# In every weight step, the matmuls that read rounded weights run first, and the wait for the weights' remainder moves behind them

## The chip, the cores and the metric

One Trainium2 chip, of which the kernel uses one core. The metric is the device time of one execution in microseconds (us): the median of several runs, lower is better. The profile describes one further execution of the same program.

## The reference

One layer of a streaming encoder for 256 tokens of width 4096, in float32. The input is normalised and multiplied by one large matrix `w_in` (4096 x 21504) whose columns feed two branches: attention in a sliding window of chunks with 16 heads, and an HGRN2 gated recurrence with 16 heads. Each branch has a SiLU gate. Both are projected up to the model width, merged by sigmoid gates, projected once more, added to the input and normalised:

```python
h = rmsnorm(x, norm_gain[l])
proj = jnp.einsum('bsd,dn->bsn', h, w_in[l])
qa, ka, va, za, qb, fb, ib, zb, ga, gb = jnp.split(proj, SPLIT_POINTS, axis=-1)
a = window_sink_attention(qa, ka, va, attn_sinks[l]) * jax.nn.silu(za)
ob = hgrn2_chunkwise(qb, fb, ib, lower_bounds[l])
...
y = (jax.nn.sigmoid(ga) * jnp.einsum('bsc,cd->bsd', a, w_up_attn[l])
     + jax.nn.sigmoid(gb) * jnp.einsum('bsc,cd->bsd', b, w_up_hgrn[l]))
x = x + jnp.einsum('bsd,de->bse', y, w_out[l])
return rmsnorm(x, final_norm_gain)
```

Nearly all of the work is in these matrix products: some 0.5 GB of weights are read once.

## The kernel before, in words

**Weight steps.** All products with large matrices are cut into weight steps. A step takes one tile of weights, 128 rows of the contraction by 512 columns, and multiplies it with all 256 tokens. There are 1856 steps, numbered through the whole program. To keep the precision of float32 with the faster float32r matmul, both operands are split into a rounded part and a remainder, and a step makes three products: rounded by rounded, remainder of the activations by rounded weights, rounded activations by the weights' remainder. The tokens are two tiles of 128 (`TT` = 2, the stationary operand `l_hi` or `l_lo`), the weights are the moving operand (`w_hi`, `w_lo`, 512 columns). So a step is six matmuls (`step_r`, lines L399 to L401), each accumulating into one PSUM bank of 512 columns per token tile; 16 or 32 steps fill one output block of 512 columns.

**How a tile of weights gets there.** SyncE (SP) fetches two tiles with one DMA into the ring `raw` of four slots (`load_steps`, L316). ScalarE (ACT) copies a tile with rounding to `w_hi` (`round_step`, L596) and signals `hi_ready`; it waits for the DMA and for TensorE to have finished the step four places earlier (`pe_done`), since `w_hi` and `w_lo` are rings of four (`RING`). VectorE (DVE) waits for `hi_ready`, subtracts `w_hi` from `raw` and writes `w_lo` (`rest_step`, L856), and signals `lo_ready`. TensorE (PE) waits for `lo_ready` before the first matmul of the step. `lo_ready` also lets SP refill `raw`.

**What stands between the steps.** Every engine has one queue in order, and the program writes by hand at which step k of a block which side work goes. TensorE transposes finished rows (`turn`, L411), and makes the small matmuls of the heads. In an HGRN head (32 steps; `hgrn_side`), TensorE computes level scores behind k = 14 and k = 18 (L419, L421) and the head's output behind k = 22 (L441 to L443), for which it waits for `att_done`, among others. VectorE masks the scores at k = 16 and 20 (L927) and sums them in one long reduction `at_m` at k = 17 and 21 (L934), behind the `rest_step` of the same k. There are 16 such heads in four groups; their side work runs beside the steps numbered 128 to 639. After them come keys and values, the attention heads (16 steps each), the merge with its gates and up projections, and the output projection (`project`), which adds the residual. In its first block VectorE also makes `h_lo` of the merged rows (L1138).

**Signals of a step.** The last matmul of a step signals `pe_done`. In the last step of a block of the output projection, the third product of token tile 0 also signals `tile0_done`, so that VectorE can add the residual of that half (`residual`, L1122) while the second half is still being multiplied. In the blocks within the projection the residual stands behind `rest_step` of k = 3 of the next block; the last block's residual stands behind nothing but the wait. After it come squares (L831), the final norm and the stores.

**Loops.** The first HGRN group and some blocks between phases are written out; the rest runs in loops, 16 iterations in all. In a loop the value that a wait compares with depends on the iteration: `count` gives an expression of the loop's register, and the engine works it out with a register instruction.

**In the diff:** `step_t` is a second form of the step, called from nowhere. `step_r` is called by `hgrn_group`, the last HGRN block, `attn_blocks`, `merge` and `project`.

Of the kernel before, what the change touches and what calls it, by code (L numbers as in the profile page):

```python
# [30 lines left out]
P = 128  # L31
# [7 lines left out]
SEQ = 256  # L39
TT = SEQ // P  # L40
D = 4096
KT = D // P
HD = 128
HEADS = 16
KVH = 4
GH = 4
# [3 lines left out]
BLK = GH * HD  # L50
# [41 lines left out]
RING = 4  # L92
# [13 lines left out]
def count(base, per=0, it=0):  # L106

    def c(k=0, unit=1):
        if isinstance(it, int):
            return (base + per * it + k) // unit  # L110
        assert per % unit == 0
        return it * (per // unit) + (base + k) // unit
    return c


def build(nc, x, norm_gain, w_in, attn_sinks, lb_logits, hgrn_norm_gain, w_up_attn, w_up_hgrn,
          w_out, final_norm_gain, tables, out):
    ctx = ExitStack()
    with ctx:
        def sb(name, shape, dt=F32):  # L120
            return ctx.enter_context(nc.sbuf_tensor(name, shape, dt))

        def sem(name):
            return ctx.enter_context(nc.semaphore(name))
# [3 lines left out]
        w_hi = sb("w_hi", [P, RING, BLK], F32R)  # L128
        w_lo = sb("w_lo", [P, RING, BLK], F32R)
# [78 lines left out]
        acc = ctx.enter_context(nc.psum_tensor("acc", [P, 2, 2 * BLK], F32))  # L208
# [6 lines left out]
        hi_ready = sem("hi_ready")  # L215
        lo_ready = sem("lo_ready")
        pe_done = sem("pe_done")
# [154 lines left out]

        @block.tensor
        def _(pe):
            def step_t(n, k, par, r_hi, r_lo, kt, last, free):

                s = k % RING
                if kt == 0 and free is not None:
                    pe.wait_ge(*free)
                pe.wait_ge(lo_ready, n(k + 1))  # L380
                for c in range(GH):
                    o = acc[:, par, c * SEQ:(c + 1) * SEQ]
                    cols = slice(c * HD, (c + 1) * HD)
                    first = kt == 0 and c % 2 == 0
                    nc.tensor.matmul(o, w_hi[:, s, cols], r_hi[:, kt, :], start=first, stop=False)
                    nc.tensor.matmul(o, w_hi[:, s, cols], r_lo[:, kt, :], start=False, stop=False)
                    m = nc.tensor.matmul(o, w_lo[:, s, cols], r_hi[:, kt, :], start=False, stop=last and c % 2 == 1)
                m.then_inc(pe_done, 1)

            def step_r(n, k, par, l_hi, l_lo, kt, last, free, rows_done=None):  # L390

                s = k % RING
                if kt == 0 and free is not None:
                    pe.wait_ge(*free)
                pe.wait_ge(lo_ready, n(k + 1))
                for t in range(TT):
                    o = acc[:, par, t * BLK:(t + 1) * BLK]
                    tok = slice(t * P, (t + 1) * P)
                    nc.tensor.matmul(o, l_hi[:, kt, tok], w_hi[:, s, :], start=kt == 0, stop=False)  # L399
                    nc.tensor.matmul(o, l_lo[:, kt, tok], w_hi[:, s, :], start=False, stop=False)  # L400
                    m = nc.tensor.matmul(o, l_hi[:, kt, tok], w_lo[:, s, :], start=False, stop=last)  # L401
                    if last and t == 0 and rows_done is not None:
                        m.then_inc(rows_done, 1)
                m.then_inc(pe_done, 1)
# [82 lines left out]
            def hgrn_group(n, g, hd, nt, side):  # L487


                before = [(i_copied, g), (silu_done, g * 2), (sig_f_done, g + 1), (silu_done, g * 2 + 1)]  # L490
                for b in range(4):
                    free = before[b] if side or b >= 2 else None
                    for k in range(KT):
                        kk = b * KT + k
                        if not side and b == 0 and k % 2 == 0:
                            pe.wait_ge(h_lo_done, k // 2 + 1)
                        step_r(n, kk, b % 2, h_hi, h_lo, k, k == KT - 1, free)
                        if k == 16 and (side or b) and b < 3:

                            turn((b - 1) % 2, turn_h, nt(b))  # L500
                        if side:
                            hgrn_side(k, lambda i, b=b: hd(b + i))
                        elif b == 0 and k % 2 == 0 and k // 2 + 3 < KT // 2:
                            input_pair(k // 2 + 3)
# [10 lines left out]
            n = count(N_HG)  # L515
            before = [(i_copied, GROUPS), (silu_done, 2 * GROUPS), (kv_copied, 1), (kv_copied, 2)]
            for b in range(4):
                for k in range(KT):
                    kk = b * KT + k
                    free = before[b]  # L520
                    step_r(n, kk, b % 2, h_hi, h_lo, k, k == KT - 1, free)
                    if k == 16 and b != 2:
                        turn((b - 1) % 2, turn_h, 3 * GROUPS + {0: 0, 1: 1, 3: 2}[b])
                    hgrn_side(k, lambda i, b=b: (GROUPS - 1) * GH + b + i)


            def attn_blocks(n, hd, g, nt):
                before = [(qa_copied, g + 1), (silu_done, g + (2 * GROUPS + 1))]
                for b in range(2):
                    for k in range(KT):  # L530
                        kk = b * KT + k
                        step_r(n, kk, b % 2, h_hi, h_lo, k, k == KT - 1, before[b])
                        if k == 7:

                            turn((b - 1) % 2, turn_a, nt(b + 1))
                        attn_side(k % 16, lambda i, u=kk // 16: hd(u + i), g)
# [681 lines left out]
```

## Time and profile before

| | us |
|---|---|
| median of 3 runs | 2707.37 |
| lowest and highest | 2707.24, 2707.83 |
| the profiled execution, its own time | 2707.25 |
| its span, first to last instruction | 2704.7 |
| TensorE busy in matmuls (PE) | 2672.3 |
| weight loads (PEld, beside PE) | 2219.0 |
| VectorE busy (DVE) | 1609.3 |
| ScalarE busy (ACT) | 1452.1 |

Times on the timeline count from the span's start. A timeline row gives start, duration, engine, line and operation, and in brackets how long the engine was idle before and what released it; "x3" is several like instructions in a row. PE are the matmuls, PEld the loads of the stationary operand, which run beside the matmul before. The end of a matmul is modelled and matmuls are pipelined, so their rows overlap: each lasts 0.39 us although the next starts 0.23 us after it. What a standstill costs is therefore read from the starts. "issue" is time in which an engine waited for nothing that the profile shows.

### The profile page before, as it was taken

How to read it: one execution, taken by the hardware profiler on the slowest of the kernel's cores; microseconds unless marked ns; L12 is line 12 of the kernel's file. 1: busy time of each engine (PE TensorE's matmuls, PEld its weight loads, DVE VectorE, ACT ScalarE, POOL GpSimd, SP SyncE). 2: the span in 40 equal slices, each digit the busy share in tenths (PEclk: the TensorE clock that was granted, in tenths of full speed). 3: DMA queues.
4: the chain of work that ended last, by engine and by line, in shares of the span. 5: the costliest groups of instructions: out<-in, count | busy, mean ns of one | idle time of the engine just before them, and what ended most of it. 6: DMA issues, size and time to landing. Idle time of an engine off the chain costs nothing.

```text
span 2704.7 us, 39969 instructions
## 1 busy us (share of the span) xinstructions
PE 2672.3 (99%) x12249; PEld 2219.0 (82%) x12249; DVE 1609.3 (59%) x3037; ACT 1452.1 (54%) x2418; POOL 0.2 (0%) x4
## 2 busy tenths in 40 slices
PE   8999999999999999999999999999999999999997
PEld 7888888888888888888888888888888888888886
DVE  6457777777777765555555555555555555655554
ACT  6556565565565555555654444444444444554444
POOL 0000000000000000000000000000000000000000
PEclk9999999999999999999999999999999999999999
DMA  7665555565555556656666666666666666666665
GB/s 238 193 187 171 162 175 168 163 179 163 164 178 157 175 168 178 178 171 180 177 189 192 194 188 192 193 190 191 193 192 189 194 188 194 203 215 204 215 213 182
DMA packets 258914, 503.06 MB, mean 186 GB/s; under 512 B 15552, under 2 KB 15760, under 8 KB 258832
## 3 DMA queue, kind: packets, MB, share of 16 engines
q1 hardware_dynamic: 258608, 502.02, 61.6%
q8 instruction: 41, 0.67, 0.1%
q14 instruction: 41, 0.34, 0.0%
q10 hardware_dynamic: 224, 0.03, 0.0%
HBM read 497.80 MB, written 4.19 MB: 186 GB/s over the span
## 4 chain that ended last, share of the span: by engine, by line
PE 95%; DVE 2%; issue 1%; DMA 0%; ACT 0%; SPq 0%; DVEq 0%; ACTq 0%
PE acc L399 30%; PE acc L401 30%; PE acc L400 30%; PE lev L419 1%; DVE lev_m L927 1%; DVE w_lo L856 1%; PE acc L411 1%; DVE at_m L934 1%; PE lev L421 0%; DMA x_in<-in_x_dram 0%; PE lev L547 0%; PE mis L447 0%; PE mis L432 0%; PE lev L456 0%; PE mis L461 0%
## 5 line engine op out<-in xcount | busy, mean ns | idle before, releaser
L856 DVE TENSOR_TENSOR w_lo<-raw,w_hi 128x512 fp32r<-128x512 f32 x1856 | 1260.7, 689 | 918.7 <-ACT w_hi L596 918.3
L596 ACT ACTIVATE w_hi<-raw 128x512 fp32r<-128x512 f32 x1856 | 1146.9, 630 | 1027.6 <-PE acc L401 1012.3
L399 PE MATMUL acc<-w_hi,h_hi 128*128 128x512 f32 x3200 | 1267.3, 396 | 7.2 <-DVE w_lo L856 6.4
L401 PE MATMUL acc<-w_lo,h_hi 128*128 128x512 f32 x3200 | 1247.9, 390 | 0.0
L400 PE MATMUL acc<-w_hi,h_lo 128*128 128x512 f32 x3200 | 1246.4, 390 | 0.0
L399 PEld LDWEIGHTS acc<-w_hi,h_hi 128*128 128x128 f32 x3200 | 601.4, 188 | 136.2 <-DVE w_lo L856 14.9
L401 PEld LDWEIGHTS acc<-w_lo,h_hi 128*128 128x128 f32 x3200 | 600.9, 188 | 127.8
L400 PEld LDWEIGHTS acc<-w_hi,h_lo 128*128 128x128 f32 x3200 | 601.5, 188 | 120.3
L399 PE MATMUL acc<-w_hi,a_hi 128*128 128x512 f32 x256 | 99.6, 389 | 0.0
L400 PE MATMUL acc<-w_hi,a_lo 128*128 128x512 f32 x256 | 99.6, 389 | 0.0
L401 PE MATMUL acc<-w_lo,a_hi 128*128 128x512 f32 x256 | 99.6, 389 | 0.0
L399 PE MATMUL acc<-w_hi,b_hi 128*128 128x512 f32 x256 | 99.6, 389 | 0.0
L400 PE MATMUL acc<-w_hi,b_lo 128*128 128x512 f32 x256 | 99.6, 389 | 0.0
L401 PE MATMUL acc<-w_lo,b_hi 128*128 128x512 f32 x256 | 99.6, 389 | 0.0
L934 DVE TENSOR_REDUCE at_m<-lev_m 128x128 f32<-128x1024 f32 x32 | 63.8, 1993 | 0.0
L927 DVE TENSOR_TENSOR lev_m<-mis,tab 128x64 f32<-128x64 f32 x32 | 7.2, 225 | 89.1 <-PE lev L421 89.1
L399 PEld LDWEIGHTS acc<-w_hi,b_hi 128*128 128x128 f32 x256 | 48.1, 188 | 10.0
L399 PEld LDWEIGHTS acc<-w_hi,a_hi 128*128 128x128 f32 x256 | 48.1, 188 | 10.0
L400 PEld LDWEIGHTS acc<-w_hi,a_lo 128*128 128x128 f32 x256 | 48.1, 188 | 10.0
L400 PEld LDWEIGHTS acc<-w_hi,b_lo 128*128 128x128 f32 x256 | 48.1, 188 | 10.0
L401 PEld LDWEIGHTS acc<-w_lo,a_hi 128*128 128x128 f32 x256 | 48.1, 188 | 9.9
L401 PEld LDWEIGHTS acc<-w_lo,b_hi 128*128 128x128 f32 x256 | 48.1, 188 | 9.9
(156 smaller groups left out, 1067.8 us busy)
## 6 DMA issues: line engine op xcount, KB each, us to landing
raw<-in_w_in_dram SPq DMA_DIRECT2D x672, 512.0 KB, 3.7
raw<-in_w_out_dram SPq DMA_DIRECT2D x128, 512.0 KB, 3.9
raw<-in_w_up_attn_dram SPq DMA_DIRECT2D x64, 512.0 KB, 3.6
raw<-in_w_up_hgrn_dram SPq DMA_DIRECT2D x64, 512.0 KB, 3.6
xr<-in_x_dram SPq DMA_DIRECT2D x8, 512.0 KB, 4.6
out_dram<-xr SPq DMA_DIRECT2D x6, 512.0 KB, 4.8
x_in<-in_x_dram SPq DMA_DIRECT2D x2, 1024.0 KB, 10.7
fgain<-in_final_norm_gain_dram SPq DMA_DIRECT2D x8, 256.0 KB, 5.9
```

What stands on the lines that cost most here:

```text
L399: nc.tensor.matmul(o, l_hi[:, kt, tok], w_hi[:, s, :], start=kt == 0, stop=False)
L400: nc.tensor.matmul(o, l_lo[:, kt, tok], w_hi[:, s, :], start=False, stop=False)
L401: m = nc.tensor.matmul(o, l_hi[:, kt, tok], w_lo[:, s, :], start=False, stop=last)
L411: m = nc.tensor.transpose(acc[:, par, c * SEQ + t * P:c * SEQ + (t + 1) * P], rows_sb[:, t, c * P:(c + 1) * P], ident)
L419: nc.tensor.matmul(level_scores(t, i), decay[:, i - 1, tok], late_half(decay[:, i - 1, tok], i), start=True, stop=True)
L596: nc.scalar.activation(w_hi[:, k % RING, :], raw[:, (k // 2) % RING, k % 2, :], ACT.Copy).then_inc(hi_ready, 1)
L856: nc.vector.tensor_tensor(w_lo[:, k % RING, :], raw[:, (k // 2) % RING, k % 2, :], w_hi[:, k % RING, :].bitcast(F32), ALU.subtract).then_i ...
L927: nc.vector.tensor_tensor(late_half(lev_m[:, i, :], i), level_scores(t, i), own, ALU.mult)
L934: nc.vector.tensor_reduce(at_m[:, t, :], lev_m[:, :, :].rearrange("p l t -> p t l"), AX_X, ALU.add).then_inc(att_done, 1)
```

## The change

The unused `step_t` goes. In `step_r` the wait for `lo_ready` ahead of the six matmuls becomes a wait for `hi_ready`. The order of the matmuls changes: first, for token tile 0 and then for tile 1, the two that read `w_hi`; then the wait for `lo_ready`; then the two that read `w_lo`, tile 0 and tile 1. `tile0_done` stays on the `w_lo` matmul of tile 0, which is now the fifth and not the third, `pe_done` on the last. Nothing changes on the other engines.

```diff
         def _(pe):
-            def step_t(n, k, par, r_hi, r_lo, kt, last, free):
+            def step_r(n, k, par, l_hi, l_lo, kt, last, free, rows_done=None):
 
                 s = k % RING
                 if kt == 0 and free is not None:
                     pe.wait_ge(*free)
-                pe.wait_ge(lo_ready, n(k + 1))
-                for c in range(GH):
...
-                m.then_inc(pe_done, 1)
-
-            def step_r(n, k, par, l_hi, l_lo, kt, last, free, rows_done=None):
-
-                s = k % RING
-                if kt == 0 and free is not None:
-                    pe.wait_ge(*free)
-                pe.wait_ge(lo_ready, n(k + 1))
-                for t in range(TT):
-                    o = acc[:, par, t * BLK:(t + 1) * BLK]
-                    tok = slice(t * P, (t + 1) * P)
+                outs = [(acc[:, par, t * BLK:(t + 1) * BLK], slice(t * P, (t + 1) * P)) for t in range(TT)]
+                pe.wait_ge(hi_ready, n(k + 1))
+                for o, tok in outs:
                     nc.tensor.matmul(o, l_hi[:, kt, tok], w_hi[:, s, :], start=kt == 0, stop=False)
                     nc.tensor.matmul(o, l_lo[:, kt, tok], w_hi[:, s, :], start=False, stop=False)
+                pe.wait_ge(lo_ready, n(k + 1))
+                for t, (o, tok) in enumerate(outs):
                     m = nc.tensor.matmul(o, l_hi[:, kt, tok], w_lo[:, s, :], start=False, stop=last)
                     if last and t == 0 and rows_done is not None:
                         m.then_inc(rows_done, 1)
```

## Rows read from the trace of the kernel before

**Rows 1.** The page: busy time by engine, and the granted clock in 40 slices

```profile
PE 2672.3 (99%) x12249; PEld 2219.0 (82%) x12249; DVE 1609.3 (59%) x3037; ACT 1452.1 (54%) x2418; POOL 0.2 (0%) x4
...
PEclk9999999999999999999999999999999999999999
```

**Rows 2.** The page: the chain that ended last; a costly group of instructions

```profile
PE 95%; DVE 2%; issue 1%; DMA 0%; ACT 0%; SPq 0%; DVEq 0%; ACTq 0%
PE acc L399 30%; PE acc L401 30%; PE acc L400 30%; PE lev L419 1%; DVE lev_m L927 1%; DVE w_lo L856 1%; PE acc L411 1%; DVE at_m L934 1%; PE lev L421 0%; DMA x_in<-in_x_dram 0%; PE lev L547 0%; PE mis L447 0%; PE mis L432 0%; PE lev L456 0%; PE mis L461 0%
...
L856 DVE TENSOR_TENSOR w_lo<-raw,w_hi 128x512 fp32r<-128x512 f32 x1856 | 1260.7, 689 | 918.7 <-ACT w_hi L596 918.3
```

**Rows 3.** Timeline of TensorE's matmuls: start us, us, engine, line, operation; two stretches

```profile
120.21 0.39 PE L399 MATMUL acc<-w_hi,h_hi 128*128 128x512 f32 x1
...
121.57 0.39 PE L399 MATMUL acc<-w_hi,h_hi 128*128 128x512 f32 x1
...
1499.97 0.39 PE L399 MATMUL acc<-w_hi,h_hi 128*128 128x512 f32 x1
...
1501.33 0.39 PE L399 MATMUL acc<-w_hi,h_hi 128*128 128x512 f32 x1
```

**Rows 4.** List of waits: engine, line <- releaser: us in total, times, longest us

```profile
PEld acc L399 <- DVE w_lo L856: 14.9, 21, 0.7
...
PE acc L399 <- DVE w_lo L856: 6.4, 21, 0.3
...
PEld lev L483 <- DMA x_in<-in_x_dram: 4.2, 1, 4.2
...
PEld acc L399 <- issue: 1.8, 2, 1.2
```

**Rows 5.** Waits of the weight loads, from 200 to 400 us

```profile
PEld acc L399 <- DVE w_lo L856: 3.6, 5, 0.7
```

**Rows 6.** Instructions of line L934: count, ns min/median/max, first and last start

```profile
L934 DVE TENSOR_REDUCE at_m<-lev_m x32: 1976/2000/2004, 221.1 to 976.6; 128x128 f32<-128x1024 f32 x32
```

**Rows 7.** Timeline of step k = 22 of one head, all engines

```profile
228.88 2.00 DVE L934 TENSOR_REDUCE at_m<-lev_m 128x128 f32<-128x1024 f32 x1
...
230.80 1.88 DVE L856 TENSOR_TENSOR w_lo<-raw,w_hi 128x512 fp32r<-128x512 f32 x3
230.83 0.39 PE L401 MATMUL acc<-w_lo,h_hi 128*128 128x512 f32 x1
231.53 0.19 PEld L399 LDWEIGHTS acc<-w_hi,h_hi 128*128 128x128 f32 x1 [0.74 <-DVE w_lo L856]
231.53 0.50 PE L399 MATMUL acc<-w_hi,h_hi 128*128 128x512 f32 x1 [0.31 <-DVE w_lo L856]
...
231.87 0.40 PE L400 MATMUL acc<-w_hi,h_lo 128*128 128x512 f32 x1
```

**Rows 8.** Timeline of step k = 18 of the last head of a group

```profile
373.28 0.50 PE L399 MATMUL acc<-w_hi,h_hi 128*128 128x512 f32 x1 [0.29 <-DVE w_lo L856]
```

**Rows 9.** Timeline of two places in the output projection

```profile
2344.94 0.47 PE L399 MATMUL acc<-w_hi,h_hi 128*128 128x512 f32 x1 [0.23 <-DVE w_lo L856]
...
2345.25 0.39 PE L400 MATMUL acc<-w_hi,h_lo 128*128 128x512 f32 x1
...
2424.64 0.39 PE L401 MATMUL acc<-w_lo,h_hi 128*128 128x512 f32 x1
...
2424.90 0.50 PE L399 MATMUL acc<-w_hi,h_hi 128*128 128x512 f32 x1
```

**Rows 10.** Timeline of VectorE behind the last weight step

```profile
2688.46 1.29 DVE L1122 TENSOR_TENSOR xr<-xr,acc 128x512 f32<-128x512 f32 x2 [3.47 <-PE acc L401]
```

**Rows 11.** Timeline: weight loads of eight transposes; the next weight load starts at 1006.44

```profile
1005.44 1.03 PEld L411 LDWEIGHTS acc<-tab,turn_a 128*128 128x128 f32 x8
```

**Rows 12.** Timeline of the first weight step of the kernel

```profile
13.27 0.63 PE L400 MATMUL acc<-w_hi,h_lo 128*128 128x512 f32 x1
13.70 0.63 PE L401 MATMUL acc<-w_lo,h_hi 128*128 128x512 f32 x1
```

More of the change, by code:

```diff
@@ L374, in _ @@
         def _(pe):
-            def step_t(n, k, par, r_hi, r_lo, kt, last, free):
-                s = k % RING
-                if kt == 0 and free is not None:
-                    pe.wait_ge(*free)
-                pe.wait_ge(lo_ready, n(k + 1))
-                for c in range(GH):
[L382 to L387, printed above, removed]
-                m.then_inc(pe_done, 1)
             def step_r(n, k, par, l_hi, l_lo, kt, last, free, rows_done=None):
```

## The prediction

> **What bounds the kernel now.** I read the page's busy table and its 40 slices first: TensorE is busy for 99% of the span, at a granted clock of nine tenths or more in every slice, while VectorE has 59% and ScalarE 54% [rows 1]. The chain that ended last says the same of the order: 95% of the span lies on TensorE, 90% on the three matmul lines of the weight step [rows 2]. So only two things can move the time: how fast matmuls follow each other, and the moments at which TensorE stands still. A matmul's row lasts 0.39 us, but its end is modelled and the rows overlap, so the pace is in start times. In the timeline a matmul of 512 columns starts 0.23 us after the one before it; six of them, one weight step, take 1.36 us (120.21 to 121.57) [rows 3]. 1856 steps of 1.36 us are 2524 us of the 2704.7 us span.
>
> The standstills are in the list of waits. For the weights' remainder TensorE waited 21 times: 14.9 us by its weight loads, 6.4 us by its matmuls, at most 0.7 us at once [rows 4]. The longest single one of all is 4.2 us, for the input at the very start [rows 4]. Neither total is the cost: the weight load normally starts a matmul early, so its wait counts that lead too, and the matmul's begins only at a modelled end of 0.39 us. The cost is again in start times, below.
>
> **What the change removes.** A step now waits for w_lo before its first matmul, though only the third and sixth read it. After the change the first four wait for w_hi alone, and the wait for w_lo stands 4 x 0.23 = 0.91 us later. Where w_lo is late by less, nothing waits.
>
> Between 200 and 400 us there are five [rows 5], and the three stretches of 200 us up to 1000 us have five each too: twenty in all, where the HGRN heads run. Each head has two VectorE reductions at_m of 2.0 us (32 for 16 heads [rows 6]), and VectorE's queue is in order, so the next w_lo stands behind them. In one head the second reduction runs from 228.88 to 230.88; the w_lo behind it starts by about 230.8 and takes 1.88/3 = 0.63 us or a little more; TensorE, whose last matmul started at 230.83, starts the next at 231.53 [rows 7]. That is 0.70 us where 0.23 is usual, so 0.47 lost. The next start comes at 231.87, 0.34 us later: the weight load for it could not be brought forward either, another 0.11. After that the spacing is 0.23 again. One such wait costs **0.58 us**. Each of the 16 heads has one like it, at its step k = 22. Four more, one per group of heads, stand behind the first reduction (k = 18): there the matmul stood idle for 0.29 us behind the modelled end of the one before it [rows 8], where it is 0.31 in [rows 7], so I take 0.02 less, 0.56 us. Sum: 16 x 0.58 + 4 x 0.56 = **11.5 us**.
>
> Two stand in the output projection [rows 9]. The matmul at 2344.94 was idle for 0.23 us behind a modelled 0.39, 0.62 from start to start, and the next starts at 2345.25, 0.31 later: (0.62 - 0.23) + (0.31 - 0.23) = 0.47 us. From 2424.64 to 2424.90 it is 0.26, which with the 0.11 behind it is 0.14 us. Together **0.6 us**; 12.1 us in all.
>
> Does the later wait really pass? Without the stall the step of [rows 7] would start at 231.06, its fifth matmul at 231.97, and that matmul's weight load one matmul earlier, at 231.74. TensorE saw w_lo by 231.53. So 0.2 us is left over even for the weight load, and for k = 18 slightly more. The w_hi that now stands first is there: a w_lo is the difference of raw and w_hi, and the three w_lo from 230.80 follow each other without a pause (1.88 us for three [rows 7]), so their w_hi had been waiting. The next thing to be late is att_done, which the small matmuls behind that step need: the reduction ends at 230.88 and they would start at 232.4, so 1.5 us are left. The w_lo of the following step comes 0.6 us after the late one and is needed at least 1.36 us later. VectorE, with 59% busy, catches up from there as it does now.
>
> **What it moves.** In the last step of an output block the third matmul of token tile 0 signals tile0_done. It goes from third to fifth place: 2 x 0.227 = 0.45 us later. Within the projection the residual that waits for it stands behind a w_lo that needs the whole block finished, so nothing changes there. At the very end nothing covers it: VectorE, idle for 3.47 us before, begins the residual at 2688.46 when TensorE's line L401 lets it, and runs its two instructions in 1.29 us [rows 10]; squares, norm and stores follow one after the other. With the signal 0.45 us later, all of that moves by **+0.45 us**. pe_done keeps its place at the sixth matmul, so rounding, the refill of the weight ring and the DMA queue of SP see no change but the earlier pace; the order of accumulation alternates between the two PSUM halves more often (four changes of half per step and not two), and the existing changes are free: the start after one half's last matmul comes 0.23 us later like all others [rows 3].
>
> **What it adds.** 1856 waits for hi_ready, and in the loops a register instruction for each that works out the value. No view counts these as busy. From below: nothing, since the wait that is there costs nothing: a step in the written-out first group (120.21 to 121.57) and one in a loop, where the value is computed (1499.97 to 1501.33), both take 1.36 us [rows 3]. A gain from an added instruction is excluded. From above: TensorE's queue gets through eight weight loads and eight transposes from 1005.44 to 1006.44 [rows 11], 1.00/16 = 0.06 us an instruction. If two more per step were fully exposed, they would cost 1856 x 0.12 = some 220 us. I take nothing, by the nearest row: at 0.06 us each, the 12 instructions of a step and its wait with the register operation need 0.9 us of 1.36, and two more fit in what is left.
>
> **The sum.** -11.5 - 0.6 + 0.45 = -11.7 us. The profiled execution took 2707.25 us (span 2704.7), so 2695.6 us; the median of the runs, 2707.37, stands 0.1 us above it, which gives **2695.6** to 2695.7. About 0.2% (5.4 us, that is a bound of 2702.0) is what a measurement of this kernel tells from no change.
>
> The Trainium skill (TensorE: Matmul & The Clock Gate, section "Architectural detail: the array is 16× 32×32, not 1× 128×128") says that TensorE may pull weight loads ahead of running matmuls. If that reached past a semaphore wait, the load in [rows 7] would not have waited with its matmul and the 0.11 would not be part of the stall; it starts at the same 231.53 as the matmul, so here it does not, and the sum by the rule (some 2.3 us less gain, 2698) is not the one I take.
>
> **The rivals.**
> *A part of the stall stays* (chance 0.09): w_lo is in time for the matmul but the wait in the middle of a step has a restart of its own. If it cost the 0.11 of [rows 7] in the 20 heads' waits the time is 2698; if the load had to be released a further 0.3 us earlier, some 6 us of the gain would go, 2702. For it: only 0.2 us are left. Against it: the wait at a step's start shows no cost when it is met in time.
> *No change* (0.07): what is gained in a head is lost again, because VectorE is still behind and the next wait takes over, or the instruction stream pauses as it does once near 795 us, in a standstill of 1.2 us that the list calls "issue" [rows 4]. Time 2703 to 2708. Against it: 918.3 us of VectorE's idle time is spent waiting for w_hi [rows 2], so it has time to catch up between reductions.
> *Slower* (0.04): the added wait and its register instruction are not hidden in every step. It decides from 11.7/1856 = 0.006 us a step on; at one exposed instruction of 0.06 us per step it is +111 - 12, 2806 us. Against it: [rows 3], where the wait that exists adds nothing in either kind of step.
> *The clock* (0.01): TensorE's pace falls to its lower level of 1.2 GHz. The first matmuls after the idle start are 0.43 us apart and not 0.23 [rows 12]. Sixty matmuls at 0.43 would eat the gain, and all 11136 of them would give some 4900 us. The standstills of today leave every slice at nine tenths or more [rows 1], the mark of the upper level of 2.4 GHz, and the change has fewer of them. The Trainium skill (TensorE: Matmul & The Clock Gate, section "A second HAM failure mode: psum-queue depth-cycling") tells of a kernel whose cycling through PSUM banks idled TensorE briefly and let the clock swing; the changed order does cycle more, but no gap shows at a change of bank here.
>
> **How the numbers follow.** Forecast 0.79 at 2695.6. The range reaches from 2694.0 (the same sum with 1.6 us more, a few ordinary gaps or the pause near 795 us gone) to 2700.5, which takes in the nearer half of the first rival. Faster by over 0.2%: 0.79 and nearly all of 0.09, 0.88. Within: 0.07. Slower: 0.05, the last two rivals.
>
> **What would show it.** Right: the wait of line acc's weight load for w_lo gone from the list between 200 and 1000 us; TensorE's span from first to last matmul some 12 us shorter; steps still 1.36 us; the final residual starting after the fifth matmul of the last step and ScalarE's squares 0.45 us later behind it. Wrong: new waits of the third line for w_lo with a length of tenths, steps of more than 1.36 us in the loops, or standstills at the small matmuls behind k = 22 that are not there now.

## The result, and the profile after the change

| | before, us | after, us |
|---|---|---|
| median | 2707.30 (6 runs, 2706.85 to 2707.83) | 2694.57 (6 runs, 2693.36 to 2697.06) |
| the profiled execution, its own time | 2707.25 | 2693.91 |
| its span | 2704.7 | 2692.1 |

The ratio of the medians is 0.9953, with a 95% interval of 0.9942 to 0.9964: 12.7 us less, where 11.7 were forecast (2695.6).

The page of the changed kernel, with the lines that answer to [rows 1] and [rows 2]. The `w_hi` matmuls are now L383 and L384, the `w_lo` matmul L387; ScalarE's `w_hi` is L582 and VectorE's `w_lo` L842.

```profile
span 2692.1 us, 39969 instructions
...
PE 2665.9 (99%) x12249; PEld 2220.7 (82%) x12249; DVE 1608.6 (60%) x3037; ACT 1452.1 (54%) x2418; POOL 0.2 (0%) x4
...
PEclk9999999999999999999999999999999999999998
...
PE 99%; DMA 0%; ACT 0%; DVE 0%; SPq 0%; issue 0%; ACTq 0%; DVEq 0%
PE acc L383 31%; PE acc L384 31%; PE acc L387 31%; PE lev L405 1%; PE acc L397 1%; PE lev L407 0%; DMA x_in<-in_x_dram 0%; PE lev L533 0%; PE mis L433 0%; PE mis L418 0%; PE lev L442 0%; PE mis L447 0%; PE outp L428 0%; PE outp L452 0%; PE outp L453 0%; PE outp L429 0%
...
L842 DVE TENSOR_TENSOR w_lo<-raw,w_hi 128x512 fp32r<-128x512 f32 x1856 | 1259.9, 688 | 909.6 <-ACT w_hi L582 909.1
```

VectorE and ScalarE do the same work; the granted clock stays at nine tenths or more but for the last slice (an 8, of which the last 16 us lie behind the last matmul). Two things are to be seen here. TensorE's modelled busy time is only 6 us less, though the span is 12.6 us shorter: busy time does not show where the gain is, since it had been a matter of standstills. And the chain that ended last, which before had 2% on VectorE and 1% without a releaser, is 99% TensorE. VectorE's share there is now rounded to 0%.

The list of waits of the weight loads answers to [rows 4]. The wait for `w_lo`, 14.9 us in 21 times, is not in it at all:

```profile
PEld outp L458 <- DMA vrow<-in_hgrn_norm_gain_dram: 3.5, 1, 3.5
PEld lev L469 <- DMA x_in<-in_x_dram: 3.5, 1, 3.5
PEld mis L469 <- DMA x_in<-in_x_dram: 2.9, 1, 2.9
PEld acc L384 <- issue: 1.1, 1, 1.1
```

What is left is the input at the start and one pause of 1.1 us for which the profile names no cause; before, there was a like one of 1.2 us.

The timeline of the same head as in [rows 7]; the start times are this execution's own:

```profile
228.61 2.00 DVE L920 TENSOR_REDUCE at_m<-lev_m 128x128 f32<-128x1024 f32 x1
...
230.54 1.88 DVE L842 TENSOR_TENSOR w_lo<-raw,w_hi 128x512 fp32r<-128x512 f32 x3
...
230.79 0.39 PE L383 MATMUL acc<-w_hi,h_hi 128*128 128x512 f32 x1
...
231.47 0.39 PE L384 MATMUL acc<-w_hi,h_lo 128*128 128x512 f32 x1
231.48 0.41 PEld L387 LDWEIGHTS acc<-w_lo,h_hi 128*128 128x128 f32 x2
231.70 0.62 PE L387 MATMUL acc<-w_lo,h_hi 128*128 128x512 f32 x2
```

The reduction of 2.0 us is there as before, and the late `w_lo` behind it again starts before the reduction's end is over (the first of the three from 230.54). But the step starts at 230.79, with `w_hi`, and its load of the fifth matmul starts at 231.48, on the heels of the fourth matmul at 231.47: it has not waited. The `w_lo` matmuls follow at 231.70, 0.23 us later. The wait for `w_hi`, which now comes first, is met long before: ScalarE has ended this step's `w_hi` 4.6 us before the step's first matmul. The smallest such lead of all steps is 0.84 us (step 1662, in the output projection), the next 1.07 (step 6, at the start).

The end of the kernel, where [rows 10] had VectorE start 0.18 us ahead of the last matmul (2688.46 against 2688.64):

```profile
2675.36 0.61 PE L387 MATMUL acc<-w_lo,h_hi 128*128 128x512 f32 x2
2675.86 1.28 DVE L1108 TENSOR_TENSOR xr<-xr,acc 128x512 f32<-128x512 f32 x2 [3.92 <-PE acc L387]
2676.58 0.63 ACT L817 ACTIVATE sq_o<-xr 128x512 f32<-128x512 f32 x1 [3.86 <-DVE xr L1108]
```

The two `w_lo` matmuls start at 2675.36 and, 0.23 us later, at 2675.59; VectorE starts at 2675.86, now 0.27 us behind the last.

**Where the 12.6 us went**, from start times in both traces, cut at the same matmuls (counted from the kernel's first; the pieces are stretches of the same instructions):

| stretch | before, us | after, us | difference |
|---|---|---|---|
| span's start to matmul 49 (input, first steps) | 21.52 | 21.26 | -0.26 |
| matmul 49 to 4001 (to about 863 us) | 841.80 | 832.07 | -9.73 |
| 4001 to 8001 | 866.27 | 863.88 | -2.39 |
| 8001 to 10601 (all in the merge) | 585.72 | 585.72 | 0.00 |
| 10601 to the last (end of the merge, output projection) | 373.33 | 372.66 | -0.67 |
| last matmul to the span's end | 16.08 | 16.53 | +0.45 |

The four stretches between the start and the tail carry -12.8 us. The second profiled execution of the changed kernel has the same (832.03, 863.88, 585.72, 372.66 and 16.54 us). One thing in the stretch up to matmul 4001 is not the change's: every profiled execution has a pause there, ahead of the fourth matmul of step 512, the first step behind the loop over the head groups. The list puts it down to "issue". Before:

```profile
794.41 0.39 PE L401 MATMUL acc<-w_lo,h_hi 128*128 128x512 f32 x1
795.59 0.50 PE L399 MATMUL acc<-w_hi,h_hi 128*128 128x512 f32 x1 [0.78 <-issue]
```

From start to start it is 1.17 us before and 1.09 after, and between 0.76 and 1.88 us in the ten profiled executions of this study. Where stretches of different kernels are compared below, its difference is taken out first; here it leaves 9.65 of the 9.73 us to the change. In the merge, where no `w_lo` was late, nothing changed to a hundredth of a microsecond, although each of its steps has one wait more and four changes of PSUM half, not two.

### The profile page after: what moved, and what is told of

Same layout as the page of the kernel before. It is cut to its first block, busy times and chain, and to the rows that moved or that the text cites. A ratio compares the mean times of both kernels' runs of the same rounds, so it can differ in the third digit from the quotient of the medians.

```text
span 2692.1 us, 39969 instructions
## 1 busy us (share of the span) xinstructions
PE 2665.9 (99%) x12249; PEld 2220.7 (82%) x12249; DVE 1608.6 (60%) x3037; ACT 1452.1 (54%) x2418; POOL 0.2 (0%) x4
## 4 chain that ended last, share of the span: by engine, by line
PE 99%; DMA 0%; ACT 0%; DVE 0%; SPq 0%; issue 0%; ACTq 0%; DVEq 0%
PE acc L383 31%; PE acc L384 31%; PE acc L387 31%; PE lev L405 1%; PE acc L397 1%; PE lev L407 0%; DMA x_in<-in_x_dram 0%; PE lev L533 0%; PE mis L433 0%; PE mis L418 0%; PE lev L442 0%; PE mis L447 0%; PE outp L428 0%; PE outp L452 0%; PE outp L453 0%; PE outp L429 0%
## 5 line engine op out<-in xcount | busy, mean ns | idle before, releaser
L842 DVE TENSOR_TENSOR w_lo<-raw,w_hi 128x512 fp32r<-128x512 f32 x1856 | 1259.9, 688 | 909.6 <-ACT w_hi L582 909.1
L582 ACT ACTIVATE w_hi<-raw 128x512 fp32r<-128x512 f32 x1856 | 1147.1, 630 | 1024.3 <-PE acc L387 1008.2
L383 PE MATMUL acc<-w_hi,h_hi 128*128 128x512 f32 x3200 | 1265.4, 395 | 0.0
L384 PE MATMUL acc<-w_hi,h_lo 128*128 128x512 f32 x3200 | 1247.2, 390 | 0.7 <-issue 0.7
L387 PE MATMUL acc<-w_lo,h_hi 128*128 128x512 f32 x3200 | 986.9, 390 | 0.0
L387 PEld LDWEIGHTS acc<-w_lo,h_hi 128*128 128x128 f32 x3200 | 601.0, 188 | 127.2
L384 PEld LDWEIGHTS acc<-w_hi,h_lo 128*128 128x128 f32 x3200 | 601.5, 188 | 122.1 <-issue 1.1
L383 PEld LDWEIGHTS acc<-w_hi,h_hi 128*128 128x128 f32 x3200 | 601.4, 188 | 120.6
L383 PE MATMUL acc<-w_hi,a_hi 128*128 128x512 f32 x256 | 99.6, 389 | 0.0
L383 PE MATMUL acc<-w_hi,b_hi 128*128 128x512 f32 x256 | 99.6, 389 | 0.0
L384 PE MATMUL acc<-w_hi,a_lo 128*128 128x512 f32 x256 | 99.6, 389 | 0.0
L384 PE MATMUL acc<-w_hi,b_lo 128*128 128x512 f32 x256 | 99.6, 389 | 0.0
L387 PE MATMUL acc<-w_lo,a_hi 128*128 128x512 f32 x256 | 78.8, 389 | 0.0
L387 PE MATMUL acc<-w_lo,b_hi 128*128 128x512 f32 x256 | 78.8, 389 | 0.0
L383 PEld LDWEIGHTS acc<-w_hi,b_hi 128*128 128x128 f32 x256 | 48.1, 188 | 10.0
L383 PEld LDWEIGHTS acc<-w_hi,a_hi 128*128 128x128 f32 x256 | 48.1, 188 | 10.0
L384 PEld LDWEIGHTS acc<-w_hi,a_lo 128*128 128x128 f32 x256 | 48.1, 188 | 10.0
L384 PEld LDWEIGHTS acc<-w_hi,b_lo 128*128 128x128 f32 x256 | 48.1, 188 | 10.0
L387 PEld LDWEIGHTS acc<-w_lo,a_hi 128*128 128x128 f32 x256 | 48.1, 188 | 9.9
L387 PEld LDWEIGHTS acc<-w_lo,b_hi 128*128 128x128 f32 x256 | 48.1, 188 | 9.9
```

The source lines that it names most:

```text
L582: nc.scalar.activation(w_hi[:, k % RING, :], raw[:, (k // 2) % RING, k % 2, :], ACT.Copy).then_inc(hi_ready, 1)
L842: nc.vector.tensor_tensor(w_lo[:, k % RING, :], raw[:, (k // 2) % RING, k % 2, :], w_hi[:, k % RING, :].bitcast(F32), ALU.subtract).then_i ...
```

## The experiments

In the runs below the kernel before had medians of 2707.52 and 2707.62 us (15 runs in each of the two sets, 2705.6 to 2710.3), and the times are to be seen beside these.

### The changed kernel again

> The changed kernel again, beside the others on the same chip. Theory: 12.7 us below the kernel before (2707.3), so 2694.6. It is here for the spread of its runs too: six of them lay between 2693.4 and 2697.1, while those of before lay within 1 us. If the spread belongs to the new order, the kernel with the order alone has it as well; if it belongs to the chip, only some calls show it.

2694.28 us (5 runs, 2692.88 to 2696.71), ratio 0.9950 [0.9936, 0.9964]. The result stands. In this set the runs of the kernel before spread over 4.6 us, those of the changed one over 3.8: the spread is not a trait of the new order.

### The order alone

```diff
-                pe.wait_ge(hi_ready, n(k + 1))
+                pe.wait_ge(lo_ready, n(k + 1))
                 for o, tok in outs:
...
-                pe.wait_ge(lo_ready, n(k + 1))
                 for t, (o, tok) in enumerate(outs):
```

> The new order of the six matmuls, but one wait for lo_ready ahead of all of them as before. Theory (the later wait is the whole gain): the 21 standstills are back at 0.58 us each, the tail keeps its +0.45 us, so 2707.3 + 0.45 = 2707.8 us. Rival (the order itself is cheaper, for example because matmuls alternate between PSUM halves): steps shorter than 1.36 us and a time near 2695.

2708.37 us (11 runs, 2707.49 to 2709.88), ratio 1.0003 [0.9994, 1.0012]. The first row is from its waits, the others from the timeline of its end:

```profile
PEld acc L383 <- DVE w_lo L841: 14.9, 21, 0.7
```

```profile
2688.94 0.61 PE L386 MATMUL acc<-w_lo,h_hi 128*128 128x512 f32 x2
2689.44 1.28 DVE L1107 TENSOR_TENSOR xr<-xr,acc 128x512 f32<-128x512 f32 x2 [3.93 <-PE acc L386]
```

The 21 waits are back with the very total of before. At the end VectorE starts 0.27 us behind the last matmul (2688.94 + 0.23 = 2689.17), as in the changed kernel. So the order by itself gains nothing, costs nothing per step (its merge stretch takes 585.72 us too, with four changes of PSUM half a step and not two), and brings the 0.45 us of the tail. Its stretch up to matmul 4001 is 0.8 us longer than before (842.59 us), of which 0.7 is the pause at step 512, 1.88 us here. The whole gain is the place of the wait.

### The wait only ahead of the third matmul

```diff
-                pe.wait_ge(lo_ready, n(k + 1))
+                pe.wait_ge(hi_ready, n(k + 1))
                 for t in range(TT):
...
                     nc.tensor.matmul(o, l_lo[:, kt, tok], w_hi[:, s, :], start=False, stop=False)
+                    if t == 0:
+                        pe.wait_ge(lo_ready, n(k + 1))
                     m = nc.tensor.matmul(o, l_hi[:, kt, tok], w_lo[:, s, :], start=False, stop=last)
```

> The old order, wait for hi_ready first and for lo_ready only ahead of the third matmul, so w_lo may come 0.45 us later than before. Theory: of the 0.47 us of a k = 22 standstill 0.02 stays, and the matmul behind it still starts 0.11 us late because its weight load could not go ahead: 0.13 us x 16 + 0.11 x 4 + about 0.1 = 2.6 us of 12.8 stay, no change in the tail: 2707.3 - 10.2 = 2697.1 us. Rival (a weight load that is released in the middle of a step costs nothing): 0.02 x 16 stays, 2694.8 us.

2697.02 us (5 runs, 2695.87 to 2697.56), ratio 0.9960 [0.9946, 0.9974]. Its waits, and then the step k = 22 of the same head; L403 is the `w_lo` matmul:

```profile
PEld acc L403 <- DVE w_lo L858: 5.7, 20, 0.3
```

```profile
230.80 0.39 PE L400 MATMUL acc<-w_hi,h_lo 128*128 128x512 f32 x1
231.05 0.19 PEld L403 LDWEIGHTS acc<-w_lo,h_hi 128*128 128x128 f32 x1 [0.29 <-DVE w_lo L858]
231.06 0.50 PE L403 MATMUL acc<-w_lo,h_hi 128*128 128x512 f32 x1
...
231.39 0.40 PE L399 MATMUL acc<-w_hi,h_hi 128*128 128x512 f32 x1
```

The third matmul was due at 231.03 and starts at 231.06. It is hardly late, and yet the one behind it starts 0.33 us later and not 0.23, because both weight loads had been held up. That is the 0.13 us that was expected, and the first two stretches (834.12 and 864.46 us) are 2.6 us longer than those of the changed kernel, 2.9 us without the pause at step 512, which was 0.29 us shorter here. The merge stretch is 585.72 us again, the tail is back at 16.08 us. This is the finest test of the account: half the delay of the wait buys most of the gain, and what stays is the 0.1 us or a little more of late weight loads in each of 20 places.

### VectorE's reduction in two halves, the waits as before

```diff
-                if k in (17, 21):
+                if k in (17, 18, 21, 22):
...
-                    nc.vector.tensor_reduce(at_m[:, t, :], lev_m[:, :, :].rearrange("p l t -> p t l"), AX_X, ALU.add).then_inc(att_done, 1)
+                    part = slice(0, P // 2) if k in (17, 21) else slice(P // 2, P)
+                    m = nc.vector.tensor_reduce(at_m[:, t, part], lev_m[:, :, part].rearrange("p l t -> p t l"), AX_X, ALU.add)
+                    if k in (18, 22):
+                        m.then_inc(att_done, 1)
```

(and a wait of VectorE for its own `att_done` ahead of the masks of k = 20)

> The kernel before with its old waits; VectorE's long reduction at_m is cut in two halves of about 1.0 us, the second behind the rest_step of the next k, so that w_lo is not late. Theory (the standstills are VectorE's queue, not anything in TensorE): the waits for w_lo at k = 18 and 22 go, only the two in the output projection stay (0.6 us), and the tail is unchanged: 2707.3 - 12.2 = 2695.1 us, if att_done, now about 1.3 us later, is still in time (by my sum by 0.2 us). Rival (something else holds TensorE there): waits stay, 2707.

2697.06 us (5 runs, 2695.35 to 2700.15), ratio 0.9961 [0.9947, 0.9974]. Its waits for `w_lo`, and the same place of the head in its timeline:

```profile
PE acc L399 <- DVE w_lo L856: 0.2, 1, 0.2
```

```profile
229.88 1.07 DVE L937 TENSOR_REDUCE at_m<-lev_m 128x64 f32<-128x512 f32 x1
...
230.87 0.68 DVE L856 TENSOR_TENSOR w_lo<-raw,w_hi 128x512 fp32r<-128x512 f32 x1
...
231.47 1.07 DVE L937 TENSOR_REDUCE at_m<-lev_m 128x64 f32<-128x512 f32 x1
...
232.45 1.29 DVE L856 TENSOR_TENSOR w_lo<-raw,w_hi 128x512 fp32r<-128x512 f32 x2
```

Each half takes 1.07 us, and a `w_lo` stands between the two. Of the 21 waits one is left, in the output projection. The stretches up to matmul 8001 are 9.52 and 2.38 us shorter than before, next to the 9.73 and 2.39 of the change; without the pause at step 512 (1.31 us here) both have 9.65 in the first. `att_done` was in time, then. The second place of [rows 9] was not late in this execution, since ScalarE's `w_hi` came a little earlier there. So the standstills came from VectorE's queue, and they go with either remedy. The median is 1.9 us above what was expected. The profiled execution (2695.63 us) is only 0.5 us above it, less than its slower start accounts for (input and first steps, 22.53 us where it was 21.52); why the median of the five lies higher was not found.

### VectorE made later by a memset

```diff
                     t = (k - 17) // 4
+                    if t:
+                        nc.vector.memset(bb2[:, :], 0.0)
                     dve.wait_ge(masked, hd(0) * 2 + (t + 1))
```

(in the third of these kernels also a memset of `bb1`)

> The kernel before with VectorE's queue made later by one memset of 128x256 (0.25 to 0.3 us, a quarter of the 0.91 us that a memset of 128x1024 takes, and a start) ahead of the second at_m reduction of each of the 16 heads. It writes a buffer that is overwritten before it is read, so the output is unchanged. Theory (there is no slack at all, the lateness of w_lo is paid in full): 16 x 0.28 = +4.5 us, 2712 us. Rival (part of the standstill is a fixed cost): less than +2 us.

2709.22 us (11 runs, 2708.28 to 2712.88), ratio 1.0008 [0.9999, 1.0018].

```profile
228.48 0.27 DVE L934 MEMSET bb<- 128x256 f32 x1
...
228.67 1.86 DVE L936 TENSOR_REDUCE at_m<-lev_m 128x128 f32<-128x1024 f32 x1
...
231.18 0.19 PEld L399 LDWEIGHTS acc<-w_hi,h_hi 128*128 128x128 f32 x1 [0.87 <-DVE w_lo L856]
231.19 0.50 PE L399 MATMUL acc<-w_hi,h_hi 128*128 128x512 f32 x1 [0.45 <-DVE w_lo L856]
...
231.52 0.39 PE L400 MATMUL acc<-w_hi,h_lo 128*128 128x512 f32 x1
```

The memset takes 0.27 us, but the reduction behind it is recorded with 1.86 us and not 2.00, so only 0.13 us of lateness came of it: the weight load waits 0.87 us and the matmul 0.45, where [rows 7] have 0.74 and 0.31. That lateness was paid in full. The stretches up to matmul 8001 grew by 2.4 us; 0.3 of that is the pause at step 512 (1.48 us here), and the other 2.1 are 0.13 a head, the very lateness. The expected +4.5 us was wrong because the memset's length is not the delay it makes. The times (+1.6 us, by the medians) can't tell the theory from the rival's "less than +2 us"; the rows of the head and the stretches do.

> The changed kernel with the same memset. By my sum w_lo was seen 0.2 us before the weight load of the fifth matmul and 0.43 us before that matmul itself. 0.28 us more lateness eats the first margin and not the second. Theory (a load that comes late by less than a matmul's length still ends in time, the matmul decides): within 1 us of the changed kernel, 2694.5 to 2695.5 us. Rival (the weight load decides, and its 0.11 us is paid): 16 x 0.11 = +1.8 us, 2696.3 us.

2694.88 us (5 runs, 2693.09 to 2695.57), ratio 0.9951 [0.9937, 0.9964].

```profile
231.08 1.87 DVE L842 TENSOR_TENSOR w_lo<-raw,w_hi 128x512 fp32r<-128x512 f32 x3
...
231.88 0.39 PE L384 MATMUL acc<-w_hi,h_lo 128*128 128x512 f32 x1
231.88 0.41 PEld L387 LDWEIGHTS acc<-w_lo,h_hi 128*128 128x128 f32 x2
232.11 0.62 PE L387 MATMUL acc<-w_lo,h_hi 128*128 128x512 f32 x2
```

No wait for `w_lo`: the load of the fifth matmul starts with the fourth matmul (231.88), the fifth 0.23 us later. What costs 2.1 us in the old form costs nothing in the new one: the first stretch is 832.61 us, and 0.56 us longer only by the pause (1.65 us here), so 832.05 where the changed kernel has 832.07. With 0.13 us and not 0.28, though, the lateness stayed within the 0.2 us of the load, so this run does not tell my two cases apart. The next one does.

> The changed kernel with two such memsets (about 0.5 us). Now w_lo is seen 0.07 to 0.1 us after the fifth matmul was due. Theory: 0.1 us of lateness and the 0.11 us of the load behind it, in 16 heads: +3 us, 2697.6 us, and 16 waits for w_lo by the w_lo matmul's load. Rival (the margin is the full 0.91 us behind the step's start, counted from when w_lo was late before): no cost, 2694.6 us.

2695.58 us (5 runs, 2694.86 to 2696.58), ratio 0.9954 [0.9941, 0.9968].

```profile
230.26 1.87 DVE L842 TENSOR_TENSOR w_lo<-raw,w_hi 128x512 fp32r<-128x512 f32 x3
...
230.78 0.39 PE L384 MATMUL acc<-w_hi,h_lo 128*128 128x512 f32 x1
230.99 0.30 PEld L387 LDWEIGHTS acc<-w_lo,h_hi 128*128 128x128 f32 x2 [0.24 <-DVE w_lo L842]
231.00 0.71 PE L387 MATMUL acc<-w_lo,h_hi 128*128 128x512 f32 x2
```

Now `w_lo` is some 0.4 us later than in the changed kernel (0.54 us of memsets less the same 0.13). The fourth matmul started at 230.78, the load behind it should have started then too and starts at 230.99; 16 such waits, 3.9 us in the list. The fifth matmul starts at 231.00, just in time. But the two together last 0.71 us and not 0.62: the sixth is 0.09 us late. So the margin of a late operand ends at the weight load, 0.2 us behind the lateness of today; beyond it 0.08 to 0.09 us a head is due even while the matmul is in time, some 1.3 us in all (833.40 and 864.13 us in the first two stretches, where the changed kernel has 832.07 and 863.88, less 0.29 us of a longer pause). The expected 3 us counted 0.1 us of lateness of the matmul itself, which did not come.

### Tile 0 first in the last step of an output block

```diff
+                by_tile = last and rows_done is not None
...
+                    if by_tile:
+                        if t == 0:
+                            pe.wait_ge(lo_ready, n(k + 1))
+                        m = nc.tensor.matmul(o, l_hi[:, kt, tok], w_lo[:, s, :], start=False, stop=True)
+                        if t == 0:
+                            m.then_inc(rows_done, 1)
```

> The changed kernel, but the last step of each output projection block has the old order (tile 0's three matmuls, then tile 1's), with the wait for w_lo ahead of the third. Theory: the tail is 0.45 us shorter, VectorE begins the last residual before the last matmul starts as it did before (0.18 us ahead of it) and not 0.27 us behind it; 2694.1 us, a difference from the changed kernel that the times alone can hardly show and the profile's starts can. Rival (the tail is set by the second residual and not by the first): no difference in the span behind the last matmul.

2694.84 us (5 runs, 2693.96 to 2695.53), ratio 0.9951 [0.9938, 0.9965]. The end of the kernel, and one row of its waits:

```profile
2676.63 1.30 DVE L1114 TENSOR_TENSOR xr<-xr,acc 128x512 f32<-128x512 f32 x2 [3.47 <-PE acc L389]
2676.82 0.39 PE L389 MATMUL acc<-w_lo,h_hi 128*128 128x512 f32 x1
2677.35 0.63 ACT L823 ACTIVATE sq_o<-xr 128x512 f32<-128x512 f32 x1 [3.40 <-DVE xr L1114]
```

```profile
PEld acc L384 <- ACT w_hi L588: 1.9, 1, 1.9
```

VectorE starts 0.18 us ahead of the last matmul again, and from the last matmul to the span's end it is 16.08 us, against 16.53 to 16.55 in all five profiled executions with the changed order in the last step. The 0.45 us of the tail is therefore real and avoidable. In the time it can't be seen: 0.45 us is less than the spread of the runs, and this execution lost more than that to a late `w_hi` at step 1662 (374.38 us in the output projection's stretch, where the changed kernel has 372.66). It is the better form by the trace, and not shown to be faster by the times.

## Why the prediction was right

**What bounds the kernel.** Right. Matmuls in a stream start 0.23 us apart in every kernel of this study, and the only thing that could move was the standstills.

**What the change removes.** The place and the cause are shown from both sides: the waits are gone in the changed kernel, return to the same 14.9 us with the order alone, and vanish also when VectorE's reduction is cut. The size was 12.1 us by my sum and is 12.8 by the stretches. The missing 0.7 us is in three small things, of which only the first is wholly the change's. The matmuls after a standstill are spaced a few hundredths more than 0.23 for some steps, which makes a standstill 0.60 us and not 0.58 or 0.56 (2.39 us for the four of the second stretch); that gives some 0.5 us over twenty. The pause at step 512 is 1.09 us from start to start where it was 1.17, well within what it varies by. And the stretch of the output projection gave 0.67 us, not 0.6; the smaller of its two places, 0.14 us at 2424.90, is step 1662, where ScalarE had been idle and `w_lo` was late for that reason. How late differs from one execution to the next: the stretch was 373.17 to 373.33 us in the four profiled executions that wait for `w_lo` first.

**"0.2 us is left over even for the weight load."** Right, and the number that the result hung on: in the changed kernel the `w_lo` of a step k = 22 ends 0.48 us before its matmul at the closest, which is 0.2 us before the load, with the 0.05 us that TensorE takes to see it. The rival that a part of the stall stays had its mechanism right: a wait that is met too late does cost 0.1 us behind it, seen at a step's start in [rows 7], and in the middle of a step with the wait at the third matmul and with two memsets. It did not decide because the fifth place has the margin that the third lacks.

**What it moves.** +0.45 us was forecast, +0.45 came, and order_only and tile0_third add and take it away alone.

**What it adds.** The cost of nothing is right, one step of its working is not. I had a register instruction with every added wait. The page counts 39969 instructions before and after, and TensorE's register operations (1483 of them) are the same; the wait for the other semaphore with the same value needs none. My argument that two would fit beside the matmuls was thus never put to the test. What is shown is that the wait itself is free where it is met in time: 585.72 us for 2600 matmuls of the merge, with one wait a step or with two.

**The other rivals.** VectorE does catch up: no later wait took over. The clock did not move (0.998 granted before, 0.997 after), although PSUM half changes more often; what the Trainium skill tells in "A second HAM failure mode: psum-queue depth-cycling" (TensorE: Matmul & The Clock Gate) did not appear here. What the Trainium skill says of weight loads pulled ahead of running matmuls (same page, "Architectural detail: the array is 16× 32×32, not 1× 128×128") holds between waits: in the changed kernel's head above the load starts at 231.48, with the matmul before its own. Every held-up load in this study shows that it ends at a wait that is not met, as in [rows 7].

The median lies 1.0 us below the forecast; the 0.7 us above are the greater part of it. The rest is within the spread of the runs, of which the start has its share: from the span's start to matmul 49 the profiled executions took 20.6 to 22.5 us, whatever the kernel.

## What to carry to other kernels

Put a wait directly ahead of the first instruction that needs what it waits for, and order independent instructions so that the ones whose operand comes late are last; where one engine feeds another through a queue in order, a single long instruction there sets how much room is needed, not the busy shares (VectorE was at 59%). Read the cost of a standstill from start to start, including the instruction behind it: the list gave 14.9 us by one engine row and 6.4 by the other, and it was 12. Leave room for the weight load as well as for the matmul, and look at what a moved signal does where nothing follows that covers it.

## What was not expected of the hardware

A reduction of 128x1024 elements was recorded with 2.00 us behind a `w_lo` and with 1.86 us behind a memset, so that 0.27 us of added work made its successor only 0.13 us later. TensorE pauses once in every profiled execution with no releaser, always ahead of the fourth matmul of step 512, for 0.76 to 1.88 us from start to start. ScalarE stands idle in all ten ahead of the `w_hi` of step 1662, two steps before the loop of the output projection: for 3.1 to 3.3 us in eight of them, and for 5.0 and 5.5 us in two (the one with two memsets and the one with tile 0 first). In the kernel before:

```profile
2423.49 2.22 ACT L596 ACTIVATE w_hi<-raw 128x512 fp32r<-128x512 f32 x4 [3.22 <-issue]
```

In the two with 5.0 and 5.5 us TensorE waited for `w_hi` and started that step 1.1 and 1.6 us late. Both have the new order, but so have four of the eight others, and with the old wait it would have been later by the 0.7 us that `w_lo` ends behind `w_hi` at this step. What makes these pauses was not tried.
